# Gate and up products of eight feed-forward chunks formed transposed, two token tiles at once

## What is computed

```
def swiglu(h, w_gate, w_up, w_down):
    return (jax.nn.silu(h @ w_gate) * (h @ w_up)) @ w_down

def modulated_sublayer(x, mod, g, b, fn, res_w):
    shift, scale, gate = mod[:, 0, None, :], mod[:, 1, None, :], mod[:, 2, None, :]
    y = fn(x * (1.0 + scale) + shift)
    return layer_norm(DEEPNORM_ALPHA * x + res_w * (1.0 + gate) * y, g, b)
```

## Time and profile before

| what | value |
|---|---|
| median of 3 executions | 1115.54 us (1113.69 to 1116.57) |
| the profiled execution, its own time | 1113.41 us |
| its span, first to last instruction | 1111.6 us |
| PE busy | 1024.0 us, 92% of the span |
| DVE busy | 805.9 us, 72% |
| ACT busy | 488.5 us, 44% |
| POOL busy | 70.0 us, 6% |
| mean granted TensorE clock | 0.967 of full speed |
| moved by DMA | 255.32 MB, mean 230 GB/s |

### The profile page before, as it was taken

The page is one execution under the profiler, slowest core; times in us unless marked ns, Lnnn a source line. Parts: engine busy times, 40 slices in busy tenths (PEclk is TensorE's granted clock), DMA queues, the critical chain, the costliest instruction groups (busy, mean ns, idle before and its releaser), DMA issues.

```text
span 1111.6 us, 13098 instructions
## 1 busy us (share of the span) xinstructions
PE 1024.0 (92%) x5004; PEld 850.8 (77%) x5004; DVE 805.9 (72%) x1135; ACT 488.5 (44%) x684; POOL 70.0 (6%) x172
## 2 busy tenths in 40 slices
PE   1799999989896989999998999999988898999996
PEld 1688888879875778888887888888777777888884
DVE  5898888867675578788777878877755567566455
ACT  2444344366555354434434443443455535434440
POOL 0000000001201000000000000000431000000001
PEclk9899999989987999999998999999899899999998
DMA  9999999447122469979848898972223329556530
GB/s 365 390 393 356 327 378 366 163 145 244 33 85 86 152 233 333 337 278 335 296 151 304 309 319 272 382 252 98 77 80 114 114 80 360 203 202 216 208 114 38
DMA packets 72319, 255.32 MB, mean 230 GB/s; under 512 B 8768, under 2 KB 10048, under 8 KB 72256
## 3 DMA queue, kind: packets, MB, share of 16 engines
q1 hardware_dynamic: 68944, 243.43, 61.2%
q0 software_dynamic: 3168, 10.52, 2.7%
q10 hardware_dynamic: 144, 0.52, 0.1%
HBM read 253.37 MB, written 1.07 MB: 229 GB/s over the span
## 4 chain that ended last, share of the span: by engine, by line
PE 52%; issue 8%; DVE 7%; ACT 4%; POOL 2%; DMA 2%; POOLq 0%; SPq 0%; ACTq 0%; DVEq 0%
PE bank L1400 16%; PE bank L1404 15%; PE bank L1403 15%; ACT w_hi L689 2%; DMA w_raw<-in_w_dram 2%; PE bank L1723 1%; PE bank L1496 1%; DVE w_lo L936 1%; POOL arena L647 1%; PE bank L1601 1%; PE bank L1519 1%; DVE arena L1031 1%; DVE arena L1282 1%; PE bank L1486 1%; DVE stats L1044 1%
## 5 line engine op out<-in xcount | busy, mean ns | idle before, releaser
L936 DVE TENSOR_TENSOR w_lo<-w_raw,w_hi 128x2048 fp32r<-128x2048 f32 (+2 forms) x164 | 360.3, 2217 | 61.8 <-ACT w_hi L689 61.8
L1400 PE MATMUL bank<-w_hi,hT_hi 128*128 128x512 f32 (+3 forms) x880 | 357.7, 406 | 31.8 <-DVE hT_lo L963 14.9
L1403 PE MATMUL bank<-w_hi,hT_lo 128*128 128x512 f32 (+3 forms) x880 | 346.8, 394 | 0.0
L1404 PE MATMUL bank<-w_lo,hT_hi 128*128 128x512 f32 (+3 forms) x880 | 346.8, 394 | 0.0
L689 ACT ACTIVATE w_hi<-w_raw 128x2048 fp32r<-128x2048 f32 (+2 forms) x164 | 303.7, 1856 | 34.6 <-DMA w_raw<-in_w_dram 27.3
L1400 PEld LDWEIGHTS bank<-w_hi,hT_hi 128*128 128x128 f32 x880 | 170.9, 194 | 64.8 <-issue 20.7
L1404 PEld LDWEIGHTS bank<-w_lo,hT_hi 128*128 128x128 f32 x880 | 170.9, 194 | 35.5
L1403 PEld LDWEIGHTS bank<-w_hi,hT_lo 128*128 128x128 f32 x880 | 171.5, 195 | 30.9
L944 DVE SCALAR_TENSOR_TENSOR arena<-arena,c_row 128x1024 f32<-128x1024 f32 x144 | 171.0, 1219 | 9.8 <-DMA arena<-in_ada_w_dram 9.6
L736 ACT ACTIVATE arena<-bank 128x256 f32<-128x256 f32 x88 | 33.7, 383 | 317.1 <-PE bank L1404 317.1
L1400 PE MATMUL bank<-w_hi,fT_hi 128*128 128x512 f32 x352 | 137.7, 391 | 0.9 <-DVE fT_lo L1339 0.9
(11 more groups left out here) (201 smaller groups left out, 825.6 us busy)
## 6 DMA issues: line engine op xcount, KB each, us to landing
w_raw<-in_w_dram SPq DMA_DIRECT2D x310, 512.0 KB, 5.4
arena<-in_ada_w_dram SPq DMA_DIRECT2D x144, 512.0 KB, 6.9
gate_row<-gate_scratch POOLq DMA_DIRECT2D x6, 512.0 KB, 4.8
arena<-in_ln_g_dram POOLq DMA_DIRECT2D x6, 512.0 KB, 5.1
arena<-in_ln_b_dram POOLq DMA_DIRECT2D x6, 512.0 KB, 7.2
w_raw<-in_w_dram SPq DMA_DIRECT2D x8, 256.0 KB, 2.8
w_raw<-in_w_dram SPq DMA_DIRECT2D x8, 192.0 KB, 2.8
out_dram<-x SPq DMA_DIRECT2D x2, 512.0 KB, 2.7
```

The source lines that it names most:

```text
L936: nc.vector.tensor_tensor(w_lo[:, j0 % RING, 0:n], w_raw[:, j0 % RAW, 0:n], w_hi[:, j0 % RING, 0:n].bitcast(F32), ALU.subtract)\
L1400: mm = nc.tensor.matmul(dst, a_hi, b_hi, start=start, stop=False)
L1403: nc.tensor.matmul(dst, a_lo, b_hi, start=False, stop=False)
L1404: return nc.tensor.matmul(dst, a_hi, b_lo, start=False, stop=stop)
```

## The change

The eight chunks 1 to 8 (units 2 to 17) are handled whole. `up_wide` forms gate and up transposed: the weights are stationary, 128 columns at a time, and the 256 tokens of both tiles move. The gate of a chunk goes to one bank and the up part to another, each holding two blocks of 128 hidden columns by 256 tokens; two pairs of banks alternate, made of the former `G` and `T` banks. A chunk is 8 feature blocks by 2 (gate, up) by 2 (column blocks) by 3 matmuls. As the hidden values come out with the hidden columns on the partitions, they need no `turn`; `silu`, `hidden`, `take_hi` and `take_lo` each become one instruction of 512 words per partition, the last two read `hid` in SBUF. `down_wide` does the same 24 matmuls as the two `down` calls before. PE's order becomes up_wide(i+2), down_wide(i). `take_hi` now waits till PE has given back the down slot of the chunk before, since `fT_hi` holds only one chunk. Chunks 0, 9 and 10 stay as they were. The tables of slots and pieces merge two units in one step; the scale and shift of `x` and the angle table on VectorE move to the nearest even step.

```
+        STEPS = (0, 1, *range(2, 18, 2), 18, 19, 20, 21)
+        def wide(i):
+            return 2 <= i < 18
         def mid_slots(i):
-            c, t = UNITS[i]
-            if i == 0 or i > 17:
-                return []
-            return [3 * (c + 1) + 2 if t else 3 * (c + 1)]
+            return [3 * (i // 2) + 4] if wide(i) else [5] if i == 1 else []
         def end_slots(i):
-            c, t = UNITS[i]
-            if i < 17:
-                return [] if t else [3 * (c + 1) + 1] if i else [3, 4]
-            return {17: [30, 31], 18: [32], 19: [33]}.get(i, [])
+            if wide(i):
+                n = 3 * (i // 2) + 5
+                return [n, n + 1] if i < 16 else [n, n + 1, n + 2]
+            return {0: [3, 4], 1: [6], 18: [32], 19: [33]}.get(i, [])
...
+        def wide_banks(i):
+            return (G[i // 2 % 2 ^ 1], T[i // 2 % 2 ^ 1])
...
                     def silu(i):
+                        if wide(i):
+                            act.wait_ge(gu_done, ffn_units[s] + i + 2)
+                            nc.scalar.activation(sg[:, :, :], wide_banks(i)[0][:, :].rearrange("p (q n) -> p q n", q=2),
+                                                 ACT.Silu).then_inc(silu_done, 2)
+                            return
...
                     def take_hi(i):
-                        act.wait_ge(hid_tr, ffn_units[s] + i + 1)
+                        if wide(i):
+                            j = base[s] + 3 * (i // 2) - 1
+                            act.wait_ge(hid_ready, ffn_units[s] + i + 2)
+                            act.wait_ge(slot_free[j % RING], j // RING + 1)
+                            nc.scalar.activation(fT_hi[:, :, :], hid[:, :, :], ACT.Copy).then_inc(fT_hi_ready, 2)
+                            return
...
                     def hidden(i):
+                        if wide(i):
+                            dve.wait_ge(silu_done, ffn_units[s] + i + 2)
+                            nc.vector.tensor_tensor(hid[:, :, :], sg[:, :, :], wide_banks(i)[1][:, :]
+                                                    .rearrange("p (q n) -> p q n", q=2), ALU.mult).then_inc(hid_ready, 2)
+                            return
...
+                    def up_wide(i):
+                        c = i // 2
+                        pe.wait_ge(hid_ready, ffn_units[s] + max(i - 2, 1))
+                        for k in range(KD):
+                            j0 = base[s] + 3 * c + k // 4
+                            if k % 4 == 0:
+                                slot_wait(j0)
+                            for v, bank in enumerate(wide_banks(i)):
+                                for q in range(2):
+                                    w = slice((k % 4) * 512 + v * 256 + q * P, (k % 4) * 512 + v * 256 + (q + 1) * P)
+                                    dst = bank[:, q * SEQ:(q + 1) * SEQ]
+                                    hi, lo = w_hi[:, j0 % RING, w], w_lo[:, j0 % RING, w]
+                                    for n, (a, b) in enumerate(((hi, hT_hi), (hi, hT_lo), (lo, hT_hi))):
+                                        mm = nc.tensor.matmul(dst, a, b[:, k, :], start=k == 0 and q == 0 and n == 0,
+                                                              stop=k == KD - 1 and n == 2, skip_group_check=True)
+                            if k == 3:
+                                mm.then_inc(freed(j0), 1)
+                        mm.then_inc(gu_done, 2)
+                    def down_wide(i, frees):
+                        c = i // 2
+                        j0 = base[s] + 3 * c + 2
+                        pe.wait_ge(fT_ready, ffn_units[s] + i + 2)
+                        slot_wait(j0)
+                        for t in range(NT):
+                            for half in range(2):
+                                for q in range(2):
+                                    w = slice(q * D + half * 512, q * D + half * 512 + 512)
+                                    mm = product(Y[t][half][:, :], fT_hi[:, q, t * P:(t + 1) * P],
+                                                 fT_lo[:, q, t * P:(t + 1) * P], w_hi[:, j0 % RING, w],
+                                                 w_lo[:, j0 % RING, w], False, False,
+                                                 frees if t == 0 and half == 0 and q == 0 else None)
+                        mm.then_inc(freed(j0), 1)
...
-                    for i in range(LAST):
+                    turn(0)
+                    up(1, range(KD) if s > 0 else range(6, KD))
+                    down(0, frees=second_half(1))
+                    turn(1)
+                    up_wide(2)
+                    down(1, frees=freed(base[s] + 4))
+                    for i in range(2, 16, 2):
+                        up_wide(i + 2)
+                        down_wide(i, freed(base[s] + 3 * (i // 2 + 1) + 1))
+                    up(18)
+                    down_wide(16, None)
+                    for i in range(18, LAST):
                         turn(i)
```

More of the change, by code:

```diff
@@ L302, in pieces_of @@
             assert a == end
-            return n
+            return {i: (*n.get(i, ()), *(n.get(i + 1, ()) if wide(i) else ())) for i in STEPS}
         HG = [(512, 256), (2304, 512), (768, 512), (1280, 512), (1792, 512), (0, 512), (2816, 512)]
@@ L489, in _ @@
                     pieces = pieces_of(s)
-                    for i in range(20):
+                    for i in STEPS[:-2]:
                         if s == 0 and i == 1:
@@ L495, in _ @@
                         todo = pieces.get(i, ())
+                        if wide(i):
+                            for n in mid_slots(i):
+                                behind_lo(n)
                         for a in todo[:2]:
                             behind_piece(a)
-                        for n in mid_slots(i):
+                        for n in () if wide(i) else mid_slots(i):
                             behind_lo(n)
@@ L738, in take_hi @@
                     def take_hi(i):
-                        act.wait_ge(hid_tr, ffn_units[s] + i + 1)
+                        if wide(i):
[4 more added lines that the diff above has]
+                            return
+                        act.wait_ge(hid_tr, 6 * (ffn_units[s] // (2 * NCH)) + (i + 1 if i < 2 else i - 15))
                         nc.scalar.activation(fT_hi[:, i % 2, :], T[i % 2][:, 0:CW], ACT.Copy).then_inc(fT_hi_ready, 1)
-                    for i in range(LAST + 1):
+                    for i in STEPS:
                         if s == 0 and i == 0:
@@ L1337, in take_lo @@
                     def take_lo(i):
+                        if wide(i):
+                            dve.wait_ge(fT_hi_ready, ffn_units[s] + i + 2)
+                            nc.vector.tensor_tensor(fT_lo[:, :, :], hid[:, :, :], fT_hi[:, :, :].bitcast(F32),
+                                                    ALU.subtract).then_inc(fT_ready, 2)
+                            return
                         dve.wait_ge(fT_hi_ready, ffn_units[s] + i + 1)
@@ L1350, in _ @@
                         todo = pieces.get(i, ())
+                        if wide(i):
+                            for n in mid_slots(i):
+                                split_lo(base[s] + n)
                         for a in todo[:2]:
@@ L1705, in up @@
                             elif k == 0:
[L1706 removed]
+                                pe.wait_ge(hid_ready, ffn_units[s] + (i - 2 if i == 18 else i - 1))
                             if k % 4 == 0 and t == 0:
```

13 lines of the change are left out of this document (7 added, 6 removed).

## The result

The changed kernel takes 1116.84 us (median of 7 runs, 1114.07 to 1119.64), the kernel before in the same comparison 1113.79 us (7 runs, 1112.26 to 1116.57). The ratio is 1.0036, with a 95% interval of [1.0019, 1.0052]: 4.0 us slower (2.1 to 5.8). The ratio is not the quotient of the two medians, which lie 3.05 us apart. That is more than no change at all, and about what this kernel's measurement can tell. Executions of one kernel also differ with their mean granted clock, those at 0.970 or more being some 3 us shorter than those at 0.968 or less, but the difference stands at either (in experiment 1, whose kernel runs as long as the changed one, the medians are 1115.61 for 1111.29 us of before at the higher clock and 1118.73 for 1114.35 at the lower).

A forecast was written before the change was run, and what follows sets the result against it. PE's gapless matmul stream at full clock was taken as the bound. Per chunk +0.64 -0.54 gave +0.095, +3.0 us over 32 chunks, less a 0.6 stall: +2.4, median 1115.54 to 1117.9 us; likeliest case 1116 to 1120.5, range 1110 to 1128.

The forecast's parts named there:

- The distance of a narrow matmul, 0.1200 from the mixer: In up_wide on PE, 256-column matmuls start 0.1200 us apart: 96 take 11.52 us a chunk for 10.88 before, +0.64.
- worse-distance rival: Narrow matmuls in the feed-forwards keep 0.123 us instead of the mixer's 0.120: +9 us, 1127 us; chance 13%.
- A `turn` for 0.27 us: Each pair of transposes on PE costs 0.27 us, 0.14 itself, the rest slow-starting matmuls behind; two gone a chunk, -0.54 us.
- `down` at 5.44: The 24 down matmuls of a chunk on PE take 24 at 0.2267, 5.44 us, before and after.
- A chunk of before at 16.87: Two units of 8.433 us on PE in the first feed-forward make 16.87 us a chunk, against 16.96 after.
- ACT, DVE and the loads at nothing: Edits to ACT, DVE and DMA cost nothing, covered by PE's 11.52 us of up_wide.
- DVE's step of the first feed-forward: DVE needs 15 us of work in each chunk's 16.96 us and so does not set the pace.
- The stall of unit 18, -0.6 us: In the second feed-forward PE loses 0.62 us before unit 18's transposes; the longer down_wide before them removes it, -0.6 us.
- the 0 to 0.5 us in the first feed-forward: DVE's `hidden` of unit 18 may come late for PE's transposes, stalling once by 0 to 0.5 us; taken as 0.
- The sum, +2.4 us: Whole kernel: +3.0 us over 32 chunks less 0.6 for the stall, profiled execution 1113.4 to 1115.8 us.
- Cheaper matmuls: In up_wide a stationary block used twice in succession saves 13 ns: 13.6 us in all, 1104.3 us, faster; chance 13%.
- A new wait: In the middle chunks, waits in ACT's queue or DVE's step replace the transposes; 0.5 us in 8 chunks, +8, 1126; chance 12%.

The follow-up runs named there:

- experiment 1: The changed kernel with the last two products of a k block exchanged, so no two successive matmuls share a stationary block; 1116.82 us, ratio 1.0035 to the kernel before.
- experiments 2: The kernel before with each 512-wide gate and up matmul of units 2 to 17 split into two 256-wide ones; 1130.75 us, ratio 1.0158.
- experiment 5: The changed kernel's order and tables on all engines, but with the matmuls of before and a chunk's four transposes in one burst; 1112.46 us, ratio 0.9990 to before.
- experiment 3: The kernel before without the transposes of units 2 to 17, so it omits a step the result needs; 1097.33 us, ratio 0.9868.
- experiment 4: The kernel before with the transposes of units 2 to 17 issued twice; 1123.78 us, ratio 1.0108.
- first pair: The first profiled executions of the changed kernel and of the kernel before; spans 1115.1 and 1111.6 us.
- second pair: Unchanged copies of the changed kernel and of the kernel before, profiled once more, one execution each; 1114.22 and 1110.01 us.

## Why the prediction was right, step by step

The forecast was 1117.9 us, measured were 1116.84: +0.22% foretold, +0.36% [+0.19%, +0.52%] found. The forecast started from a median of before of 1115.54 over three executions; over seven it is 1113.79, so the forecast time is 1.1 us too high while the forecast change, +2.4 us, is smaller than the measured one. It said "slower" with 0.45 and "no change" with 0.42, and the result lies on the line between them. The mechanism was right: one more fixed part per matmul against the transposes saved, all on PE's path. That the sum agrees so well is in part luck, as the item on the sum shows.

- **The distance of a narrow matmul, 0.1200 from the mixer.** Measured 0.1199 in all four feed-forwards. The worse-distance rival (0.123) falls with 3072 matmuls on record. That the width alone carries the cost is shown by experiments 2 and 5.
- **A `turn` for 0.27 us.** Right as a whole: experiment 3 gives 8.43 - 8.16 = 0.27. Wrong in its parts: the 0.14 "for itself" is what the rows show between two starts, but by number a pair costs 0.215 (experiment 4). A distance between two starts hides what is pushed into the ones behind it. For the sum of this change it made no difference, as both parts went together.
- **`down` at 5.44.** 5.47: a wide matmul behind narrow ones starts slowly, 0.24 at 111.13 to 111.37. This is the missing 0.02 us of the chunk (16.98 for 16.96), 0.6 us over 32 chunks.
- **A chunk of before at 16.87.** Read from the first feed-forward alone; in the other three it is 16.84 to 16.85, another 0.5 us over 24 chunks.
- **ACT, DVE and the loads at nothing.** Right inside the eight chunks, where PE waits for none of them, and experiment 5, with the same order, is no slower than before. DVE's step of the first feed-forward was put at 15 us; its terms add up to 14.4, and the rows after agree (143.72 of 170.00 us is 14.4 of 16.98). At the edge of the chunks a wait of before is missing in the changed kernel; see the item on the sum.
- **The stall of unit 18, -0.6 us.** Right, and the 0 to 0.5 us in the first feed-forward came out at 0.19.
- **The sum, +2.4 us.** From the transposes of unit 1 to those of unit 18 the feed-forwards are 1.04, 0.46, 1.02 and -0.16 us longer: +2.36. Two misses of about 1 us cancel in this. Without waits the four are 0.85, 1.08, 1.02 and 1.07 us longer, 4.0 in all where +3.0 was forecast (the two items on `down` and on the chunk of before). Against it stands a wait that the prediction did not name: in before one unit of the last feed-forward takes 9.66 us, from 927.69 to 937.35, as PE waits for `fT` of unit 1:

```profile
934.49 0.50 PE L1400 MATMUL bank<-w_hi,fT_hi 128*128 128x512 f32 x1 [0.89 <-DVE fT_lo L1339]
```

In before once more the unit is 9.28 us, with 0.51 of idle, and in experiment 3 PE idles there for 1.60; experiments 2 and 4, with the same order, show no such wait, and neither does the changed kernel in two executions. So it varies from one execution to the next; that `up_wide(2)`, twice as long as `up(2)`, covers it is a guess that no run tests. It gave -1.2 us in the first pair and -0.8 in the second, which the sum left out. In the second pair the four differences are 1.05, 0.75, 1.08 and 0.21 us, +3.1.
- **What was left out.** Nothing was said of the stretches in which no instruction changes. One of them is 1.2 to 2.1 us longer, the other two are 0.8 to 1.3 us shorter, and together they add 0.4 to 0.7 us to the feed-forwards. The longer one goes with where the granted clock falls, in all eleven traces; what makes the clock fall at that place stays open.
- **The rivals.** Cheaper matmuls: refuted by experiment 1. A new wait: refuted by the rows of after.

## What to carry to other kernels

Read the pace of a full PE from the distances between starts, for each width apart, before turning a product over: twice as many matmuls of half the width cost their fixed part again, and here it ate what the saved transposes gave (+0.64 against -0.54 us a chunk). When a transposed form lets two products share a stationary block, join them into one wider matmul rather than issue them in succession, and group matmuls of one width. That turned the same idea from 0.4% slower into 0.8% faster.

## What the runs showed of the hardware

- At full clock the distance from start to start is 0.111 us at 32 moving columns (the 24 of them that end at 788.04), 0.120 at 256 and 0.2267 at 512. The last two are columns / 2.4 GHz plus 13 ns; the first lies far above that, and as 64 columns take 0.112 us too in the mixers of before, there is a floor near 0.11. The Trainium skill ("TensorE: Matmul & The Clock Gate", "Back-to-back issue gap") gives 131 ns per matmul at 512 columns for a sustained stream with its weight loads; no stream here comes near it: the rows have 227, and for this kernel they decide.
- Loading the same stationary block twice running costs what loading another one costs: 0.120 us from start to start and 16.98 us a chunk either way (experiment 1).
- Wide matmuls start slowly behind short instructions: 0.31 us once behind a burst of transposes, and then 0.232 in the mean instead of 0.227 for some nine matmuls; behind 256-wide ones 0.23 to 0.24, without the 0.31. Alternating widths pays this every time (0.353 us a pair for 0.347, 11.29 us for the gate and up of a chunk); grouping them by eights leaves a quarter of it (11.14 us, where 11.09 would be without any).
- Two executions of one kernel differ by up to 2.1 us in a stretch where the clock falls and rises (187.91 and 185.85), and by mostly under 0.1 us in a feed-forward at full clock. In the last feed-forward of before, where a wait varies, it was 0.7. A change of 3 us is therefore better read from the stretches than from the total.
